# Expert rows of a mixture-of-experts block gathered and scattered as 64 half rows of 2 KB in place of 128 quarter rows of 1 KB

## The reference

```
logits = xt @ router_w + router_b
top_vals, top_idx = lax.top_k(logits, TOP_K)          # 4 of 32 experts
gates = softmax(top_vals)
# for each token row of expert e:
hu  = xb @ w_up[e] + b_up[e]                          # 1024 -> 2048
g   = minimum(hu[:, :D_FF], 7.0)
lin = clip(hu[:, D_FF:], -7.0, 7.0)
y   = ((lin + 1.0) * (g * sigmoid(1.702 * g))) @ w_down[e] + b_down[e]
out[token] += gate * y
```

## Time and profile before

| what | value |
|---|---|
| median of 3 runs | 3191.64 us (3191.01 to 3207.24) |
| the profiled execution's own time | 3195.7 us |
| its span, first to last instruction | 3193.9 us |
| mean granted TensorE clock | 0.930 of full speed |
| PE busy | 2815.0 us, 88% of the span |
| DVE, ACT, POOL busy | 1222.9, 787.7, 301.9 us |
| DMA moved | 583.85 MB, mean 183 GB/s |
| of it by POOL's queue (q0) | 16992 packets, 23.05 MB |

### The profile page before, as it was taken

One profiled execution on the slowest core, in us unless ns is written; L12 is line 12 of the kernel. 1 busy time (PEld: TensorE's weight loads), 2 busy tenths in 40 slices (PEclk: granted clock), 3 DMA queues, 4 the chain that ended last, 5 costly groups with the idle time before them and its releaser, 6 DMA issues. The chain is left out here.

```text
span 3193.9 us, 55735 instructions
## 1 busy us (share of the span) xinstructions
PE 2815.0 (88%) x21332; PEld 1871.3 (59%) x21333; DVE 1222.9 (38%) x2466; ACT 787.7 (25%) x1646; POOL 301.9 (9%) x391
## 2 busy tenths in 40 slices
PE   5988675999999988999967788999999687999998
PEld 4975574333333323333346566788887565778886
DVE  2236544222222222222233564433433375544433
ACT  3225321101000000011121344422323144532322
POOL 1000000222222212222201000000000100000000
PEclk8999676999999989999988899999999788999999
DMA  6234007899999999799942200122221200022221
GB/s 190 81 115 170 1 14 286 352 409 397 406 407 408 392 411 407 283 398 408 407 136 79 62 1 27 53 103 83 106 104 56 90 18 27 1 80 106 106 79 53
DMA packets 182017, 583.85 MB, mean 183 GB/s; under 512 B 31764, under 2 KB 70868, under 8 KB 132644
## 3 DMA queue, kind: packets, MB, share of 16 engines
q1 hardware_dynamic: 160708, 557.25, 44.6%
q0 software_dynamic: 16992, 23.05, 3.3%
q10 hardware_dynamic: 4098, 0.49, 0.1%
HBM read 563.17 MB, written 17.56 MB: 182 GB/s over the span
## 5 line engine op out<-in xcount | busy, mean ns | idle before, releaser
L1880 PE MATMUL moe_up<-expert_w,mod 128*32 128x512 f32 x2040 | 245.7, 613 | 28.8 <-issue 19.5
L1880 PE MATMUL moe_up<-ring,mod 128*32 128x512 f32 x1696 | 209.6, 619 | 21.2 <-DMA ring<-in_exp_w_up 16.6
L1991 DVE TENSOR_TENSOR mod<-moe_up,mod 128x512 f32<-128x512 f32 x85 | 58.8, 692 | 440.8 <-PE moe_up L1880 439.9
L361 PE MATMUL mlp_bank<-hT_hi,mlp_w 128*128 128x512 f32 x512 | 199.4, 390 | 0.0
L362 PE MATMUL mlp_bank<-hT_lo,mlp_w 128*128 128x512 f32 x512 | 199.2, 389 | 0.0
L363 PE MATMUL mlp_bank<-hT_hi,mlp_w 128*128 128x512 f32 x512 | 199.2, 389 | 0.0
L361 PE MATMUL mlp_bank<-mlp_w,mlp_u_hi 128*128 128x512 f32 x512 | 199.2, 389 | 0.0
L362 PE MATMUL mlp_bank<-mlp_w,mlp_u_hi 128*128 128x512 f32 x512 | 199.2, 389 | 0.0
L363 PE MATMUL mlp_bank<-mlp_w,mlp_u_lo 128*128 128x512 f32 x512 | 199.2, 389 | 0.0
L403 ACT ACTIVATE mlp_w<-ring 128x1024 fp32r<-128x1024 f32 x128 | 125.1, 1052 | 207.6 <-PE mlp_bank L363 207.6
L1968 ACT ACTIVATE mod<-mod 128x256 f32<-128x256 f32 x85 | 35.4, 417 | 567.6 <-DVE mod L1993 567.6
(11 more groups left out here) (506 smaller groups left out, 5501.1 us busy)
## 6 DMA issues: line engine op xcount, KB each, us to landing
expert_w<-in_exp_w_up SPq DMA_DIRECT2D x97, 1024.0 KB
ring<-in_exp_w_up SPq DMA_DIRECT2D x75, 1024.0 KB
ring<-in_w_ff SPq DMA_DIRECT2D x32, 2048.0 KB, 8.9
expert_w<-in_exp_w_down SPq DMA_DIRECT2D x47, 1024.0 KB
ring<-in_exp_w_down SPq DMA_DIRECT2D x39, 1024.0 KB
moe_w<-in_exp_w_up SPq DMA_DIRECT2D x37, 1024.0 KB
ring<-in_ada_w SPq DMA_DIRECT2D x12, 2048.0 KB, 11.5
hT<-in_exp_w_up SPq DMA_DIRECT2D x24, 1024.0 KB
```

What stands on the lines that cost most here:

```text
L361: nc.tensor.matmul(out, lhsT.hi, rhs.hi, start=(i == 0), stop=False)
L1880: mm = nc.tensor.matmul(up[quarter[q], :], rowsT[:, c % 2, quarter[c // 2]], w[:, q], start=(c == 0), stop=(c == UPS - 1))
L1991: nc.vector.tensor_tensor(pre, up[:], bias_up, ALU.add).then_inc(up_taken, 1)
```

## The change

1. A block's rows are held as two half rows each: partition p = 32 i + r, for i in 0 and 1, holds half i (512 columns, 2 KB) of row r. `rows` is now 512 columns wide on partitions 0 to 63, and `y` 512 columns wide on partitions 64 to 127. Gather and scatter move 64 pieces of 2 KB, through views of 1024 half rows.
2. `turn_rows` makes four transposes of 64 partitions x 128 columns, each against a 64 x 64 identity, in place of two of 128 x 128. The place of each 128-column slice in `rowsT` changes with it, and so do the weights' slices in `up_chunk`.
3. The PSUM quarters of `down` hold column quarters 0, 2, 1, 3 (`YPART`), so that the last multiplication can lay partitions 0 to 63 into the left and 64 to 127 into the right half of each 512-column row: DVE makes it as two instructions of 64 x 256 in place of one of 128 x 256.
4. The bias of `w_down` is loaded in two DMAs of two pieces each, in place of one of four: SP issues three small DMAs per expert and not two.
5. One semaphore increment, `rows_seen`, is added on PE behind the wait for the gather.

```diff
+HALVES = 2
+HROWS = HALVES * BR
+YPART = (0, 2, 1, 3)
...
-            chain(nc.vector.tensor_scalar(number[:], number[:], float(PARTS), k.part_no[:], ALU.mult, ALU.add))
+            chain(nc.vector.tensor_scalar(number[:], number[:], float(HALVES), k.part_no[:], ALU.mult, ALU.add))
...
-        rows, y, rowsT, hidT, sig, hid = (work[:, n, :] for n in range(6))
+        rows, y = (work[p, 0:2, :].rearrange("p a n -> p (a n)") for p in (slice(0, HROWS), slice(HROWS, P)))
+        rowsT, hidT, sig, hid = (work[:, n, :] for n in range(2, 6))
...
-        b_down = a["exp_b_down"][0].rearrange("e (q n) -> e q n", q=PARTS)
-        h2_parts = h2_dram.rearrange("s (q n) -> (s q) n", q=PARTS)
-        x_parts = x_dram.rearrange("s (q n) -> (s q) n", q=PARTS)
+        b_down = a["exp_b_down"][0].rearrange("e (i j n) -> e j i n", i=HALVES, j=HALVES)
+        h2_parts = h2_dram.rearrange("s (q n) -> (s q) n", q=HALVES)
+        x_parts = x_dram.rearrange("s (q n) -> (s q) n", q=HALVES)
...
-                sp.dma_start(bias_row[0:P:BR, UPW:], b_down[bass.ds(e, 1), :, :].rearrange("e q n -> (e q) n")).then_inc(bias_loaded, 16)
+                for j in range(HALVES):
+                    sp.dma_start(bias_row[j * HROWS:(j + 1) * HROWS:BR, UPW:], b_down[bass.ds(e, 1), j, :, :].rearrange("e i n -> (e i) n")).then_inc(bias_loaded, 16)
...
-                nc.gpsimd.tensor_copy(index[:], k.row_token[:, bass.ds(b, 1)]).then_inc(indexed, 1)
+                nc.gpsimd.tensor_copy(index[:], k.row_token[0:HROWS, bass.ds(b, 1)]).then_inc(indexed, 1)
...
-                for j in range(2):
-                    tr = nc.tensor.transpose(turn_r[:, j * P:(j + 1) * P], rows[:, j * P:(j + 1) * P], k.ident[:])
+                for j in range(ND // HALVES):
+                    tr = nc.tensor.transpose(turn_r[:, j * HROWS:(j + 1) * HROWS], rows[:, j * P:(j + 1) * P], k.ident[0:HROWS, 0:HROWS])
...
-                    mm = nc.tensor.matmul(up[quarter[q], :], rowsT[:, c % 2, quarter[c // 2]], w[:, q], start=(c == 0), stop=(c == UPS - 1))
+                    mm = nc.tensor.matmul(up[quarter[q], :], rowsT[:, c % (ND // HALVES), quarter[c // (ND // HALVES)]], w[:, q], start=(c == 0), stop=(c == UPS - 1))
...
-                        mm = nc.tensor.matmul(down[quarter[q], 0:YCOLS], hidT[:, h, quarter[at]], w[:, h, q * YCOLS:(q + 1) * YCOLS],
+                        mm = nc.tensor.matmul(down[quarter[q], 0:YCOLS], hidT[:, h, quarter[at]], w[:, h, YPART[q] * YCOLS:(YPART[q] + 1) * YCOLS],
...
                 pe.wait_ge(gathered, b * 16 + 32)
+                pe.sem_inc(rows_seen, 1)
                 turn_rows()
...
-                nc.vector.scalar_tensor_tensor(y, whole, k.row_gate[:, bass.ds(b, 1)], out_scale, ALU.mult, ALU.mult).then_inc(y_ready, 1)
+                for j in range(HALVES):
+                    p = slice(j * HROWS, (j + 1) * HROWS)
+                    scaled = nc.vector.scalar_tensor_tensor(y[:, j * YCOLS:(j + 1) * YCOLS], whole[p], k.row_gate[p, bass.ds(b, 1)], out_scale[p],
+                                                            ALU.mult, ALU.mult)
+                scaled.then_inc(y_ready, 1)
```

More of the change, by code:

```diff
@@ L1711, in _ @@
             chain(nc.vector.tensor_tensor(spare[:], spare[:], number[:], ALU.add))
-            chain(nc.vector.tensor_scalar(number[:], number[:], float(PARTS), k.part_no[:], ALU.mult, ALU.add))
+            chain(nc.vector.tensor_scalar(number[:], number[:], float(HALVES), k.part_no[:], ALU.mult, ALU.add))
             chain(nc.vector.tensor_copy(k.row_token[:], number[:]))
-            chain(nc.vector.tensor_scalar(spare[:], spare[:], float(PARTS), k.part_no[:], ALU.mult, ALU.add))
+            chain(nc.vector.tensor_scalar(spare[:], spare[:], float(HALVES), k.part_no[:], ALU.mult, ALU.add))
             chain(nc.vector.tensor_copy(k.row_place[:], spare[:]))
@@ L1758, in expert_stage @@
         work = k.mod[:, 0:2, :].rearrange("p a (b n) -> p (a b) n", n=2 * P)
-        rows, y, rowsT, hidT, sig, hid = (work[:, n, :] for n in range(6))
+        rows, y = (work[p, 0:2, :].rearrange("p a n -> p (a n)") for p in (slice(0, HROWS), slice(HROWS, P)))
+        rowsT, hidT, sig, hid = (work[:, n, :] for n in range(2, 6))
         pre = work[:, 6:8, :].rearrange("p s n -> p (s n)")
         gate, lin = pre[:, 0:YCOLS], pre[:, YCOLS:]
-        rowsT, hidT = (t.rearrange("p (h n) -> p h n", n=P) for t in (rowsT, hidT))
+        rowsT, hidT = (t.rearrange("p (h n) -> p h n", n=n) for t, n in ((rowsT, HROWS), (hidT, P)))
         hid_by_unit = hid.rearrange("p (n h) -> p h n", h=2)
-        index, place = sb("index", [P, 1], U32), sb("place", [P, 1], U32)
+        index, place = sb("index", [HROWS, 1], U32), sb("place", [HROWS, 1], U32)
         whole = k.mod[:, 3, 0:YCOLS]
@@ L1772, in expert_stage @@
         gathered, y_stored = k.gathered, k.y_stored
-        rows_turned, rows_taken = sem("rows_turned"), sem("rows_taken")
+        rows_turned, rows_taken, rows_seen = sem("rows_turned"), sem("rows_taken"), sem("rows_seen")
         up_done, down_done, up_taken, down_taken = sem("up_done"), sem("down_done"), sem("up_taken"), sem("down_taken")
@@ L1837, in scatter @@
             def scatter(b, copies, made, op=ALU.add):
-                nc.gpsimd.tensor_copy(place[:], k.row_place[:, bass.ds(b, 1)]).then_inc(indexed, 1)
+                nc.gpsimd.tensor_copy(place[:], k.row_place[0:HROWS, bass.ds(b, 1)]).then_inc(indexed, 1)
                 pool.wait_ge(indexed, copies)
@@ L1958, in take_rows @@
             def take_rows():
-                nc.scalar.activation(rowsT, turn_r[:, 0:2 * P].rearrange("p (j r) -> p j r", r=P), ACT.Copy).then_inc(rows_taken, 1)
+                nc.scalar.activation(rowsT, turn_r[:, 0:2 * P].rearrange("p (j r) -> p j r", r=HROWS), ACT.Copy).then_inc(rows_taken, 1)
             def take_hidden(b):
@@ L2015, in open_expert @@
             def open_expert(e):
-                dve.wait_ge(bias_loaded, e * 32 + 32)
+                dve.wait_ge(bias_loaded, e * 48 + 48)
                 dve.sem_inc(bias_seen, 1)
@@ L2024, in _ @@
             for q in range(PARTS):
-                nc.vector.tensor_copy(out_scale[quarter[q], :], k.mod[quarter[q], 3, q * YCOLS:(q + 1) * YCOLS]).then_inc(scale_laid, 1)
+                nc.vector.tensor_copy(out_scale[quarter[q], :], k.mod[quarter[q], 3, YPART[q] * YCOLS:(YPART[q] + 1) * YCOLS]).then_inc(scale_laid, 1)
             dve.wait_ge(scale_laid, PARTS)
```

## The result

| | before | changed |
|---|---|---|
| median of 6 runs | 3207.39 us (3191.01 to 3208.67) | 3237.1 us (3226.91 to 3239.69) |
| ratio | | 1.0104, 95% interval 1.0076 to 1.0132 |
| profiled execution, its span | 3195.7, 3193.9 us | 3239.69, 3237.9 us |
| mean granted TensorE clock | 0.930 | 0.921 |
| expert stage, first gather to last scatter | 1073.1 us | 1098.4 us |

The changed kernel is slower by 1.0%. The forecast was 3197.1 us, no change, and the range ended at 3210: both are missed.

What follows compares the result with a forecast made beforehand. The prediction took the expert stage as bound by DMA for 34 blocks and PE for 51. Transposes +8.2 and scatter -2.7 made +5.5 us, 3201.2 on the profiled execution, 3197.1 us on the median; range 3181 to 3210.

Steps and rivals of the forecast that it cites:

- nothing to gain there: Gather in the expert stage: already moved in 4 KB packets near bulk price, 0.33 us an engine, unchanged.
- signs of being wrong: PE's slot not growing, PE no longer ending the stage alone from 1277 us, or gathers showing PE waiting at L1878.
- half-path rival: Gather to partitions 0 to 63 fills half the write paths: +11.2 us, in all 3208.3 us; chance 0.16.
- What bounds the kernel: Expert stage: DMA bounds three stretches, 34 blocks; PE bounds four, 51 blocks, including 1277 to 1622 us.
- The transposes: Four small transposes on PE for two: +0.16 us a block over 51 PE-bound blocks, +8.2 us (0 to +21).
- lower bound of 0: Transposes on PE: loads of 64 partitions hide wholly and equal columns decide, so no added time.
- upper bound: Transposes on PE: two more at 0.205 us each, +0.41 us a block, +21 us in all.
- The scatter: Half as many adding packets, each 0.184 us: 0.08 us gained a block over 34 DMA-bound blocks, -2.7 us (-8.3 to 0).
- 34 blocks: Blocks counted in the three DMA-bound stretches of the expert stage, from 4494 PE records at 132 a block.
- What was costed at nothing: DVE's second instruction, third bias DMA, semaphore increment and POOL's issuing: 0, with 0.5 us either way at the stage's end.
- The base: Whole run before the change: median 3191.64 us, 4.1 below the profiled execution's 3195.7.
- likeliest case: The forecast itself for the whole run: +5.5 us, 3197.1 us, read as no change; chance 0.52.

Runs made afterwards that it cites:

- e3c: Changed kernel with y in its own tile and four 128 x 128 transposes, gather to partitions 0 to 63: stage 1102.5 us, ratio 1.0084.
- e3: Changed kernel with y in its own tile and four 128 x 128 transposes, gather to partitions 32 to 95: stage 1080.8 us, ratio 1.0034.
- e1: Changed kernel with the old gather and two transposes put back, new scatter kept: stage 1068.0 us, again 1069.8; ratio 1.0002.
- e2: Changed kernel with the old scatter and single DVE instruction put back, new gather kept, y in its own tile: stage 1103.7 us, ratio 1.0106.
- e6: Changed kernel with every gather made a second time, into partitions 0 to 63 of an unread tile: stage 1157.5 us.
- e7: Changed kernel with every gather made a second time, into partitions 32 to 95 of an unread tile: stage 1119.8 us.
- e5: Changed kernel gathering 32 whole rows of 4 KB to partitions 0 to 31, with eight transposes of 32 rows: stage 1102.6 us, ratio 1.0092.

## Why the prediction was wrong, step by step

**The step that failed.** The sum has no term for where the gather lands. It reads the gather as "near the price of bulk: nothing to gain there" and leaves its landing on 64 partitions to a rival with a chance of 0.16. The runs show this as the main cost: 21.7 us between e3c and e3, by the partitions alone. Two of the prediction's signs of being wrong came with it: PE's slot did not grow as said, and PE no longer ends the stage alone from 1277 us on. So did its sign for the half-path rival, the fall of the rate.

**What bounds the kernel: right in kind, wrong in one stretch, by an average.** The prediction read 1277 to 1622 us as one window, share 0.91, and called its 345 us PE's alone. The same trace of before, cut finer, shows it otherwise:

```profile
1277.00:1340.00 63.00, 62.68 (x690) 23.35 (x686) 15.51 (x39) 6.32 (x16) 14.03 (x20) 0.96 0.67 250
1340.00:1405.00 65.00, 64.40 (x750) 24.98 (x746) 19.36 (x49) 6.73 (x17) 16.45 (x22) 1.00 1.01 394
1405.00:1470.00 65.00, 64.41 (x742) 24.81 (x736) 17.90 (x45) 6.31 (x16) 17.95 (x23) 1.00 1.03 409
1470.00:1530.00 60.00, 58.78 (x676) 22.47 (x672) 16.24 (x41) 5.93 (x15) 15.19 (x20) 1.00 1.03 408
1530.00:1575.00 45.00, 44.60 (x520) 17.42 (x516) 14.03 (x36) 4.74 (x12) 12.10 (x16) 1.00 1.03 406
1575.00:1622.00 47.00, 44.59 (x548) 18.66 (x540) 13.33 (x33) 4.75 (x12) 12.11 (x16) 1.00 0.65 240
```

Two slack ends, 0.67 and 0.65, pull down a middle of 235 us at 1.01 to 1.03. There PE and the DMA engines were full together; PE just did not wait yet. A faster DMA would have given nothing there, as the prediction said, but a slower one uses up PE's lead: in the changed kernel PE waits for chunks at 1528.79 us. An extra DMA cost has to be counted over more stretches than a saving.

**The transposes, +0.16 us a block, +8.2 us: mis-sized.** Measured: 0.02 us a block, some 1 us in all. The pace of 0.114 us, taken from products of 128 partitions, did not hold. In the trace's instruction records the four start 0.111, 0.062 and 0.062 us after one another and the next product 0.152 us after the last; for the two of before these are 0.165 and 0.203. The lower bound of 0 (equal columns decide) was near the truth. The upper bound was misread: the eight transposes at 0.205 us ran almost wholly at half clock (first row below), and e3's transposes of 128 x 128 follow each other at 0.109 us. The 64-column products behind them ran at full clock (second row):

```profile
1804.70:1808.00 3.30, 3.02 (x12) 1.68 (x13) 2.10 (x2) 1.59 (x5) 0.00 (x0) 0.50 0.00 0
1810.00:1811.80 1.80, 1.80 (x18) 1.77 (x16) 0.79 (x3) 1.06 (x5) 0.00 (x0) 1.00 0.00 0
```

**The scatter, -0.08 us a block, -2.7 us: right for the packet, not shown on the path.** 80 packets; 0.176 us for an adding packet in the packet records, 0.184 predicted, 0.10 before. e1's lead over before is 1 to 5 us and e2's loss against the changed kernel 5.3, both of the right sign but within or near what two executions differ by. The Trainium skill, DMA: Bandwidth & Descriptors, section Specifications, was weighed there, with 512 B as the least transfer for line rate; here 2 KB as one adding packet still takes 12% less engine time than as two of 1 KB (11.5 us for 13.1).

**"Nothing to gain" in the gather: true, but only one side was asked.** That the gather moves in 4 KB packets near the price of bulk was read rightly. Whether it could become dearer was left to a rival. The 0.33 us an engine that were to stay unchanged came to 0.39, by 32 packets of 0.196 us on 16 engines, for 0.32 before in the same window.

**The half-path rival, chance 0.16, 3208.3 us: the right mechanism, too cheap.** It failed in both its factors. Its price of 0.33 us took the gather to need twice its own time, as if only its bytes were held up. Four views give more: the windows behind the 11 gathers hold on average 328 GB/s for 421, 93 x 2 us = 0.19 MB, or 0.45 us at 409; the stretch from 870 to 1000 us moves 392 for 410 (e1), 4.4% of a block of 12 us, 0.53; the packet records there have 0.38 to 0.43 us an engine more for a block's chunk packets and 0.07 for the gather's own, 0.45 to 0.50; e6 less e7 has 0.43. And its 34 blocks left out the stretch above: the changed kernel's first four windows alone hold 6126 records, at 134 a block 46 blocks. 46 x 0.46 = 21 us, an estimate from these values, against 21.7 between e3c and e3. With 1 us for PE and the saturated time between the windows this comes near the 25.3 us, but the estimate leaves out the scatter's gain and the slower clock beside the longer waits. That the sum comes out so near is partly luck.

**What was costed at nothing held, as far as shown:** DVE's second instruction, the third bias DMA and the semaphore increment are in e1 too, whose stage of 1068.0 and 1069.8 us is no longer than before's. POOL's issue at the stage's end fell by 0.14 us, not by up to 0.8.

**The base.** The sum started from a median of 3191.64 us; that of six runs is 3207.39. Of the 40 us between forecast and result some 16 are this, and 24 are what the change cost beyond the 5.5 us forecast for it. The range was drawn around a median of three as if it were firm, while one of those three already stood at 3207.24.

**The chances.** The likeliest case rested on "no row writes few partitions at such load", which is absence of evidence, and a stated rule stood against it. The half-path rival should have had a good deal more than 0.16.

## What to carry to other kernels

A small transfer beside loads that fill the DMA engines should write partitions on both sides of 64. If it can only fill 64 of them, 32 to 95 is the place and 0 to 63 or 64 to 127 are not: with the same instructions this was worth 21.7 us of 1100. In this kernel the gather to all 128 partitions stayed the fastest. Read GB/s and not only the share, since a share of 1.03 stood beside 307 GB/s and one of 1.02 beside 422. Cut a stretch finer before calling one engine its bound: where two are full together, a saving on one gives nothing, while a cost can be paid. And look up the granted clock of rows from which a pace is taken.

## What the runs showed of the hardware that was not expected

- A gather of 0.13 MB on one half of the partitions costs 0.43 to 0.53 us beyond its bytes when the DMA engines are full, more than the 0.33 us that its bytes take. It does so mostly by slowing the chunks' packets (0.31 to 0.41 us on average in the 2 us behind it) and little by its own (0.160 to 0.196). Why it is more than the time of its own bytes stays open.
- 32 partitions are no worse than 64 (1102.6 and 1102.5 us), and the upper half no better than the lower (1101.9).
- Reading from one half shows no such price: e1's scatter reads partitions 64 to 127 alone, and its stage is 1068.0 and 1069.8 us, for 1073.1 and 1069.3 before.
- Four transposes of 64 partitions and 64 columns take 0.39 us where two of 128 and 128 take 0.37. In the middle of such a group they start 0.062 us apart, and so do e5's of 32 partitions and 32 columns; those of 128 and 128 start 0.109 apart (e3), and 64-column products of 128 partitions 0.11. No run varies partitions and columns apart from each other.
- Beside waits for chunks the granted clock fell to the lower level: 6.8 us of it from 1531.2 us on, amid the waits at 1528.79 to 1534.39 us in the changed kernel, where before had neither.
- An indirect DMA's issue time on POOL hardly follows its pieces: 128 to 64 gave 1.00 to 0.94 and 1.60 to 1.44 us, and 32 pieces (e5) still a median of 0.88.
